# Second block of a two-block transformer: both row norms from one pass over h, head-norm tables built ahead, compression and its softmax moved in front of two head norms

## What is computed

```
h    = rmsnorm(x, norm1_g)            # x itself is first_block(...), which ends with its own rmsnorm(h, g_final)
proj = h @ w_in                       # 1024 -> 6308 columns
q_a,k_c,v_c,k_s,v_s,k_w,v_w,g_nsa,q_b,k_b,v_b,g_ma,g_mb = split(proj)
q_a = rope(rmsnorm(q_a, q_norm_a))    # 12 heads of 64; also k_s, k_w (3 heads), q_b, k_b (12 heads)
kc  = compress(k_c);  vc = compress(v_c)      # gelu((blocks of 32 tokens + pos) @ w1) @ w2 -> 15 blocks
kc  = rope(rmsnorm(kc, k_norm_cmp))
p   = masked_softmax(q_a @ kc * 64**-0.5)     # 24 x 15 scores per token
o_cmp = p @ vc
y_a = gate0*o_cmp + gate1*selected_attention + gate2*window_attention
y_b = dilated_attention(q_b, k_b, v_b)
x   = x + (sigmoid(g_ma)*(y_a @ w_o_a) + sigmoid(g_mb)*(y_b @ w_o_b)) @ w_out
x   = x + relu(rmsnorm(x) @ w_up)**2 @ w_down
```

## Time and profile before

| | |
|---|---|
| median of three runs | 992.61 us (991.66 to 993.39) |
| the profiled execution, its time | 992.45 us |
| its span, first to last instruction | 990.7 us |
| PE busy | 910.9 us (92%) |
| POOL busy | 680.9 us (69%) |
| DVE busy | 480.9 us (49%) |
| ACT busy | 418.2 us (42%) |
| DMA, mean | 149 GB/s |

### The profile page before, as it was taken

The page is one execution under the profiler, slowest core; times in us unless marked ns, Lnnn a source line. Parts: engine busy times, 40 slices in busy tenths (PEclk is TensorE's granted clock), DMA queues, the critical chain, the costliest instruction groups (busy, mean ns, idle before and its releaser), DMA issues.

```text
span 990.7 us, 13278 instructions
## 1 busy us (share of the span) xinstructions
PE 910.9 (92%) x5430; PEld 787.9 (80%) x5430; DVE 480.9 (49%) x677; ACT 418.2 (42%) x566; POOL 680.9 (69%) x380
## 2 busy tenths in 40 slices
PE   4979899989989999999988895989899989999998
PEld 3868787888789999997776674867677789999996
DVE  3592544243347222226399799256783444222233
ACT  4723446444244333334842443144436354333331
POOL 4967466578169999989894637540335879999984
PEclk9989999999999999999997995999799999999999
DMA  8753432444064555555851542330022553555541
GB/s 299 274 170 128 150 128 92 142 167 142 32 213 131 190 189 179 199 176 168 295 170 43 192 133 85 127 111 39 1 86 86 170 170 132 194 185 182 198 170 43
DMA packets 65490, 148.19 MB, mean 150 GB/s; under 512 B 4736, under 2 KB 10016, under 8 KB 65440
## 3 DMA queue, kind: packets, MB, share of 16 engines
q1 hardware_dynamic: 65440, 147.50, 44.1%
HBM read 146.44 MB, written 1.05 MB: 149 GB/s over the span
## 4 chain that ended last, share of the span: by engine, by line
PE 59%; DVE 17%; POOL 16%; ACT 3%; DMA 2%; issue 2%; POOLq 1%; SPq 0%; DVEq 0%; ACTq 0%
PE ps L1463 47%; POOL w_lo L559 16%; PE ps L1611 3%; DMA raw<-in_w_in 2%; PE ps L1588 2%; ACT w_hi L601 2%; PE ps L1597 1%; DVE x_lo L874 1%; DVE arena L893 1%; DVE arena L1190 1%; DVE xn L1183 1%; PE ps L1755 1%; ACT x_hi L616 1%; DVE arena L1175 1%; DVE arena L1185 1%
## 5 line engine op out<-in xcount | busy, mean ns | idle before, releaser
L559 POOL TENSOR_TENSOR w_lo<-raw,w_hi 128x512 fp32r<-128x512 f32 (+2 forms) x370 | 674.9, 1861 | 253.4 <-ACT w_hi L601 253.4
L601 ACT ACTIVATE w_hi<-raw 128x1024 fp32r<-128x1024 f32 (+2 forms) x195 | 246.4, 1323 | 304.5 <-PE ps L1463 277.7
L1463 PE MATMUL ps<-w_hi,x_hi 128*128 128x512 f32 (+1 forms) x688 | 276.7, 402 | 12.8 <-POOL w_lo L559 5.7
L1463 PE MATMUL ps<-w_lo,x_hi 128*128 128x512 f32 (+1 forms) x688 | 271.3, 394 | 0.0
L1463 PE MATMUL ps<-w_hi,x_lo 128*128 128x512 f32 (+1 forms) x688 | 270.7, 393 | 0.0
L1463 PE MATMUL ps<-x_hi,w_hi 128*128 128x256 f32 x704 | 205.1, 291 | 16.2 <-DVE x_lo L874 5.7
L1463 PE MATMUL ps<-x_lo,w_hi 128*128 128x256 f32 x704 | 201.8, 287 | 0.0
L1463 PE MATMUL ps<-x_hi,w_lo 128*128 128x256 f32 x704 | 201.7, 286 | 0.0
L1463 PEld LDWEIGHTS ps<-w_hi,x_hi 128*128 128x128 f32 x688 | 133.2, 194 | 48.0 <-issue 12.0
L1463 PEld LDWEIGHTS ps<-w_hi,x_lo 128*128 128x128 f32 x688 | 133.1, 193 | 27.4
L1463 PEld LDWEIGHTS ps<-x_hi,w_hi 128*128 128x128 f32 x704 | 137.5, 195 | 21.6 <-issue 9.5
(11 more groups left out here) (234 smaller groups left out, 766.7 us busy)
## 6 DMA issues: line engine op xcount, KB each, us to landing
raw<-in_w_in SPq DMA_DIRECT2D x36, 1024.0 KB, 5.3
raw<-in_w_up SPq DMA_DIRECT2D x32, 1024.0 KB, 5.3
raw<-in_w_down SPq DMA_DIRECT2D x32, 1024.0 KB, 4.8
raw<-in_w_xkv SPq DMA_DIRECT2D x8, 1024.0 KB, 4.9
raw<-in_w_out SPq DMA_DIRECT2D x8, 1024.0 KB, 4.8
raw<-in_w_xq SPq DMA_DIRECT2D x4, 1024.0 KB, 5.1
raw<-in_w_xo SPq DMA_DIRECT2D x4, 1024.0 KB, 4.8
raw<-in_w_o_a SPq DMA_DIRECT2D x3, 1024.0 KB, 4.8
```

The source lines that it names most:

```text
L559: x = nc.gpsimd.tensor_tensor(LO[s % 2][:, 2048 * q + d0:2048 * q + d1], RAW[n % 3][:, d0:d1], HI[s % 2][:, 2048 * q + d0:2048 * q + d1].b ...
L601: nc.scalar.activation(HI[s % 2][:, 2048 * q + c0:2048 * q + c1], RAW[n % 3][:, c0:c1], ACT.Copy).then_inc(hi_done, 1)
L1463: last = T.matmul(dst, l, r, start=start and i == 0, stop=stop and i == 2)
```

## The change

1. **Row norms 4 and 5 from one pass.** A copy `hg` = h x gain of norm 4 is made on DVE (`scaled_copy`, four operations of 128x512, two of them between the residual's additions). ACT takes the squares of h and of hg in turn and puts the first pair ahead of its `fill_hi`, the rest around the first half of `hi(IN2 + 1)`; the variance of norm 5 is worked out from the sums of hg (ss5/D + eps x m4, m4 being the mean square of norm 4 plus eps), so that one Ln and one Exp serve four columns and `r45` is simply the root of it. `h` is scaled by ACT (line 742, two operations), after the second half of `hi(IN2 + 1)`.
2. **Tables.** `T12` holds two sets; `head_tables(0)` and `(1)` are built in the first MLP, the others between other work; `kc_tables` likewise.
3. **Compression.** No duplicated copies: PE transposes k_c and v_c columns straight from `u2` (6 transposes in place of 12). The position term is not added to the input any more (the four operations at line 1229 go); its 16+16 columns stand in the zeroed fringes of `kcx`, go through the first product as two further rows, and are added to the result on 192 columns. The product reads its stationary operand with a stride of 16 elements, 64 columns (`kcx[:, c:c + 1009:16]`), where it read 45 neighbouring ones. Gelu and the gates use Sigmoid on ACT in place of Exp, add and reciprocal. Norm and rotation of kc are folded into tables; its squares are ACT's. `kc` is ready in the middle of strip 6.
4. **Order.** Scores stand before strip 7 on PE, the softmax before `head_norm(4)` and before the emptying of strip 7 on DVE; `head_norm(2)` moves behind the emptying of strip 4. On ACT the kc root moves ahead of `hi(IN2 + 7)`, the Exp of the softmax and the squares of head norm 4 ahead of `hi(IN2 + 9)`, its roots behind it. On PE the transposes of k_b come in the middle of strip 10.

The diff, cut to its core:

```diff
+            def squares(i, src, t):
+                link(nc.scalar.activation(sq_junk, src[:, t, :], ACT.Square,
+                                          accum_out=ss_n[:, 2 * i + t:2 * i + t + 1]))
             hi(IN2)
+            act.wait_ge(hg_ready, 2)
+            squares(4, h, 0)
+            squares(5, hg, 0)
             fill_hi()
-            hi(IN2 + 1)
             act.wait_ge(src_ready, 3)
-            norm_stats(4, h)
+            squares(4, h, 1)
+            hi(IN2 + 1, 0)
+            act.wait_ge(hg_ready, 4)
+            squares(5, hg, 1)
+            nc.scalar.activation(lams[:, 0:1], ss_n[:, 11:12], ACT.Copy).then_inc(norm_sq, 1)
+            act.wait_ge(hg_var, 2)
+            link(nc.scalar.activation(nr_n[:, 8:12], t_nr1[:, 0:4], ACT.Ln))
+            nc.scalar.activation(y0_n[:, 8:12], nr_n[:, 8:12], ACT.Exp, scale=-0.5).then_inc(norm_sq, 1)
+            hi(IN2 + 1, 1)
+            act.wait_ge(hg_var, 3)
+            for t in range(NT):
+                nc.scalar.activation(h[:, t, :], hg[:, t, :], ACT.Copy,
+                                     scale=rstd_n[:, 8 + t:9 + t]).then_inc(h_scaled, 1)
             hi(IN2 + 2)
-            act.wait_ge(src_ready, 4)
-            norm_stats(5, h)
...
+            act.wait_ge(tb_done, TB_W2)
+            act.wait_ge(hid_ready, 1)
+            nc.scalar.activation(ksq, bank(4 + (TB_W2 - 1) % 4)[0:15, 0:192], ACT.Square).then_inc(kc_sq, 1)
             act.wait_ge(kc_ss, 1)
             ...
+            hi(IN2 + 7)
             act.wait_ge(evac_done, strips[IN2 + 5]["evac"])
-            head_stats(3, QB, 12)
+            head_squares(3, QB, 12)
+            head_roots(3, 12)
             hi(IN2 + 8)
-            act.wait_ge(evac_done, strips[IN2 + 6]["evac"])
-            head_stats(4, KB, 12)
-            hi(IN2 + 9)
             act.wait_ge(cs_arg, 1)
             nc.scalar.activation(scb[:, :], scb[:, :], ACT.Exp).then_inc(cs_exp, 1)
+            act.wait_ge(evac_done, strips[IN2 + 6]["evac"])
+            head_squares(4, KB, 12)
+            hi(IN2 + 9)
+            head_roots(4, 12)
...
-            for kv, col in ((0, KC), (1, VC)):
-                for o in dup_views(cdup[:, 768 * kv:768 * kv + 768]):
-                    link(V.tensor_copy(o, u2[:, :, col:col + 192].rearrange("p t (g c) -> p t g c", g=3)))
             signal(at_ready, 1)
+            head_tables(2)
             u2_evac(3)
...
-                    link(V.tensor_tensor(at[:, 8 * th:8 * th + 8], src[:, :, :, th:th + CMP_N, 0],
-                                         bc(pe.unsqueeze(2).unsqueeze(2), [P, 8, 3, CMP_N]), ALU.add))
...
-                    last = T.matmul(dst[64 * kv:64 * kv + 45, 0:256], AT[:, 720 * kv + 45 * k:720 * kv + 45 * k + 45],
-                                    w1[kv][k], start=k == 0, stop=k == 15)
+                    c = 1024 * kv + 16 * (k // 8) + 2 * (k % 8)
+                    last = T.matmul(dst[64 * kv:64 * kv + 64, 0:256], kcx[:, c:c + 1009:16], w1[kv][k],
+                                    start=k == 0, stop=k == 15)
...
-            strip(IN2 + 6)
-            pe.wait_ge(kc_ready, 1)
+            strip(IN2 + 6, 0, 8)
+            pe.wait_ge(kc_ready, 2)
             ...
-            strip(IN2 + 7)
-            pe.wait_ge(kc_ready, 2)
+            strip(IN2 + 6, 8)
+            pe.wait_ge(kc_ready, 3)
             ...
+            strip(IN2 + 7)
             strip(IN2 + 8)
             pe.wait_ge(pc_ready, 1)
...
-            strip(IN2 + 10)
+            strip(IN2 + 10, 0, 8)
             pe.wait_ge(hn_done, 5)
             head_T(lambda pair, t: u2[:, t, KB + P * pair:KB + P * pair + P], 6)
+            strip(IN2 + 10, 8)
```

287 lines of the change are left out of this document (171 added, 116 removed).

## The result

The changed kernel takes 978.42 us (median of four, 976.14 to 982.95) where the kernel before took 992.13 beside it (988.24 to 993.39): ratio 0.988, 95% interval 0.9855 to 0.9906. It is faster, by 13.7 us where 23.6 were forecast, and lies outside the range of 965.5 to 976. A second series gave 978.77 beside 990.21 for the kernel before, ratio 0.9891 (0.9843 to 0.9939).

A forecast was written before the change was run, and what follows sets the result against it. PE was taken as the bound, standing still in waits that DVE releases and at a lower clock after idling. Terms -6.5 - 0.6 - 1.4 - 15.1 = -23.6 us took 992.45 to 968.9, median 969.0; range 965.5 to 976.

The forecast's parts named there:

- Opening, "+1.3": Opening, strips 0 to 3: strip 0 starts 1.3 us later (bounds 0.5 to 2.3), part of a 2.0 us loss.
- 523.4 instead of 529.92: Transposes of k_c, v_c, q_a: strip 4 starts at 523.4 us instead of 529.92, -6.5 us, opening included.
- Strip 4's clock, "-0.6": Start of strip 4: PE still idles some 2.5 us, lower clock given half its present price, -0.6 us.
- First product: First compression product: same time as before, 7.04 us, with the strided operand; taken as 0, upper bound +8.5 us.
- rival 1: Strided operand of the first compression product costs +5 to +8.5 us: 974 to 977.5; chance 0.13.
- Nothing for the second product: Second compression product: a wait of 3.2 us where there are 3.5; taken as 0, between -3 and +2.
- Scores, "-1.4": Scores after the second compression product: their wait of 1.09 us and the gap behind it go, -1.4 us.
- POOL ... needs 12.1 us beside head norm 4: Strip 9: POOL begins 3.2 us after strip 7's end and needs 12.1 us; within the softmax's -15.1 us.
- Rival 2: From strip 6 to 10 POOL and DVE hinder each other more than taken, +3 to +6: 972 to 975; chance 0.15.
- rival 3: Opening and clock come out better than taken, no stall in strip 1, -3 us: 966 or less; chance 0.05.
- rival 4: Slower than before: the strided operand's loads are serial, each line fetched alone, 38.7 us: 1000.7; chance 0.02.
- rival 5: Softmax doesn't get in front, ACT's kc root holding `hi(7)`; gives back some 5 us: 974; chance counted with Rival 2.

## Why the prediction was wrong

The direction and the ranking of the places were right: the softmax's move carries the gain, the waits that I said would go went, and the one for POOL in strip 9 came. The size was off by 9.4 us of the stretch: 4.0 up to strip 4, 1.5 at the second product and 4.7 behind it, less 0.8 from strip 4's clock. What failed is the overlap of POOL and DVE: POOL was given 12.1 us beside head norm 4 and took 14.4, and the tables and the `hg` products were given too little beside POOL. The clock behind the new waits was put at nothing and cost 1.6 us in strip 0 and 1.9 in strip 9. Point by point:

- **Opening, "+1.3".** It was +2.3 (11.6 to 13.9). I took 0.8 us for an `hg` product; both took 1.76, beside POOL. The value lay at my upper bound. To it came a low clock in strip 0 (12.6 us from its start to strip 1's, for 11.0), for which I had given nothing. The stall I put at strip 1's fourth step came in strip 3 (2.4 us).
- **"523.4 instead of 529.92".** Strip 4 started 4.0 us later than forecast, counted from the first addition. Two things put it there, and both came late. On DVE's side the sum over squares of head norm 0 started 1.7 us later than forecast by the same count, because strip 1 ended later; and the tables of head norm 2, "1.6 us beside POOL", took 3.5. I had read one operation at 1.32 us and did not multiply it by three. On PE's side strip 3 ended 62.3 us behind the first addition, where the forecast has 59.0: 1.0 from the later start, 1.6 from strip 0's clock, the rest from the stall. That is why the tables alone, moved away, gave only 0.6 us here. With the opening back strip 3 ended at 59.9, and strip 4 started at 65.2; the tables then remain as the limit.
- **Strip 4's clock, "-0.6".** -1.4 in the first profile; the other kernels show 11.1 to 13.0 us for it between PE's starts (12.6 before). The wait ahead of it is 2.0 us in both profiles of the changed kernel; between 530 and 534 us the granted clock is 1.00 in the first and 0.68 in the second. This term is a toss.
- **First product.** Right: 7.15 us against 7.04, and rival 1 fell. The loads, for which I had said 140 ns, against the earlier trace rows:

```profile
L1833 PEld LDWEIGHTS ps<-arena 128*64 128x64 f32 x40 | 5.6, 199 | 0.1
```

  A load of 64 columns 16 elements apart takes 199 ns where 45 neighbouring ones took 121; a full load of 128 neighbouring columns takes 191 to 197 elsewhere in this profile. They overlap, and the product doesn't show them. By the Trainium skill, "SBUF — State Buffer", "Door 1: The DMA port swizzle", a cost was to be expected; for the product the measurement says 0.1 us at most, and it decides.
- **"Nothing for the second product".** The tables took 5.3 us there instead of 3.3, the wait became 4.9. Taken out, they give 4.3 us and 1.3 more behind them.
- **Scores, "-1.4".** From the second product to strip 8 the profiles show about -0.6. The scores' wait and the gap behind it went as forecast, but the transposes of k_s and k_w behind the second product took 2.5 us for 1.6 (granted clock 0.54 between 566 and 569 us, 0.84 before). PE had waited 4.9 us ahead of that product, for 3.5.
- **"POOL ... needs 12.1 us beside head norm 4".** The step that failed most. That row lies beside the second half of head norm 4 alone (598.9 to 606.3), and two of its eight operations were long. Beside the whole norm four were, 14.4 us in sum, and cut free of it 10.2. The trace of before had the right row: POOL's eight operations beside the whole of head norm 0 (500.7 to 515):

```profile
L559 POOL TENSOR_TENSOR w_lo<-raw,w_hi 128x512 fp32r<-128x512 f32 x8 | 14.2, 1808 | 0.3 <-ACT w_hi L601 0.3
```

  With the clock (10.1 instead of 8.2 for the last part) strip 9 ended at +27.8 instead of +23.5: 4.3 us, nearly all that is missing behind the second product. What follows, 17.6 us, was as forecast (17.9).
- **Rival 2** named this mechanism, at +3 to +6 and a chance of 0.15. It came true, and larger than its price. I argued "I have taken every operation at its long form already", and that was untrue of the tables, the `hg` products and of POOL itself: the exclusion was counted on DVE's side only. Rivals 1, 3, 4 and 5 fell: the first product took 7.15 us, the opening came out worse, and strip 7 shows no wait for `hi(7)`.

**What stays open.** Where the clock falls in code that is the same in all kernels, and why DVE had to wait until POOL's list was empty in one profile and never in the twelve others, I can't say.

## What to carry to other kernels

Where two engines exclude each other for whole operations, an operation that is moved beside the other engine's work has two prices: its own wait, mostly up to one whole operation of the other for each small instruction (once here nine of them), and the time by which it holds up the other engine's queue; sum both, and take the duration from a row with the same neighbour. A gain at a place with two limits of nearly equal length shows only when both go: two edits that took POOL's limit off strip 9 gave nothing, and with DVE's taken off too the time fell by 5.3 us. Try every part of a change by itself: here the gain hung on one, and two others held 3.8 and 7.1 us that another place in the order gave back.

## What the runs showed of the hardware

- A table operation of 64 elements takes 0.21 us alone, 1.3 us beside POOL's operations of 512 columns, and beside its operations of 2048 (5.26 us each) this, in the first MLP of the changed kernel:

```profile
328.68 4.65 DVE L1183 TENSOR_TENSOR gain<-cst,small 128x64 f32<-128x64 f32 x1
```

  The length follows POOL's operation, not its own. It cost PE nothing: DVE had 9.4 us of idle time at this place before, the tables used it up and made the next copy out of PSUM 0.8 us late, and PE's waits between 290 and 460 us are for POOL alone, 0.2 us at the longest (0.3 before).
- From the loop's start to the end, which no edit touches, the profiles took 334.7 to 339.3 us. Behind the same wait of 2.7 us in the loop the kernel before shows

```profile
696.00:704.00 8.00, 6.37 (x23) 0.54 0.00 0
704.00:712.00 8.00, 8.00 (x50) 0.82 0.00 0
```

  and the changed one

```profile
680.00:688.00 8.00, 5.29 (x34) 0.80 0.00 0
688.00:696.00 8.00, 8.00 (x57) 0.98 0.00 0
```

  Up to 4.6 us between two profiles can thus come from code that nobody changed.
